# Value units first on un-normalised tiles, and the second block's post norm per token half

## What is computed

```python
def rms_norm(x, g):
    y = x * lax.rsqrt(jnp.mean(x * x, axis=-1, keepdims=True) + 1e-6)
    return y * g

# first block
u = rms_norm(h, norm_mix_g)
qa, ka, va, qk_b, vb, ob, ib, fb, ga, gb = split(u @ w_in)
...   # MoBA attention on a, chunkwise mLSTM on b; vb are the values of b
h = h + merged @ w_out
h = h + ffn(rms_norm(h, norm_ffn_g))
x = rms_norm(h, norm_final_g)

# second block
...   # three kinds of attention, gated and merged
x = x + rmsnorm(merged @ w_out_2, g_mix_post_2)
h = rmsnorm(x, g_ffn_pre_2)
gu = h @ w_ffn_in_2
f = (silu(gu[..., :2816]) * gu[..., 2816:]) @ w_ffn_out_2
x = x + rmsnorm(f, g_ffn_post_2)
```

## Time and profile before

| | |
|---|---|
| median of three runs | 1768.71 us (1766.45 to 1770.39) |
| the profiled execution | 1765.62 us, its span 1763.8 us |
| TensorE busy, weight loads busy | 1722.6 us (98%), 1360.6 us (77%) |
| VectorE, GpSimd, ScalarE busy | 855.0, 671.0, 628.8 us |

### The profile page before, as it was taken

The page is one execution under the profiler, slowest core; times in us unless marked ns, Lnnn a source line. Parts: engine busy times, 40 slices in busy tenths (PEclk is TensorE's granted clock), DMA queues, the critical chain, the costliest instruction groups (busy, mean ns, idle before and its releaser), DMA issues.

```text
span 1763.8 us, 23221 instructions
## 1 busy us (share of the span) xinstructions
PE 1722.6 (98%) x7974; PEld 1360.6 (77%) x7982; DVE 855.0 (48%) x1375; ACT 628.8 (36%) x1011; POOL 671.0 (38%) x284
## 2 busy tenths in 40 slices
PE   7999999999999999999999999999999899999998
PEld 5788776788888888888688665678888588888887
DVE  6602665583655552207497766441332565555013
ACT  5233445433322223327424555453223422222122
POOL 2444222234444444445243000224444444444443
PEclk9999999999999999999999999999999899999999
DMA  4434311123333223334332111113233132233332
GB/s 171 156 121 129 103 53 61 49 96 96 119 95 95 95 96 100 93 102 147 111 96 72 48 37 38 60 49 96 95 100 93 47 118 95 95 95 96 96 97 70
DMA packets 47345, 162.26 MB, mean 92 GB/s; under 512 B 5692, under 2 KB 7868, under 8 KB 47016
## 3 DMA queue, kind: packets, MB, share of 16 engines
q1 hardware_dynamic: 43728, 151.16, 27.1%
q10 hardware_dynamic: 3544, 10.13, 1.7%
HBM read 156.91 MB, written 4.76 MB: 92 GB/s over the span
## 4 chain that ended last, share of the span: by engine, by line
PE 66%; issue 20%; POOL 6%; DVE 5%; ACT 1%; DMA 0%; SPq 0%; POOLq 0%; DVEq 0%; ACTq 0%
PE ps L441 19%; PE ps L443 19%; PE ps L442 19%; POOL w_lo L388 6%; PE ps L908 1%; PE ps L907 1%; PE ps L909 1%; PE ps L606 1%; PE ps L627 1%; PE ps L643 1%; PE ps L795 1%; DVE tmp L1548 1%; DVE tmp L1975 1%; PE ps L837 0%; DMA w_raw<-stream 0%
## 5 line engine op out<-in xcount | busy, mean ns | idle before, releaser
L388 POOL TENSOR_TENSOR w_lo<-w_raw,w_hi 128x1024 fp32r<-128x1024 f32 x267 | 658.5, 2469 | 1066.2 <-ACT w_hi L978 1066.2
L441 PE MATMUL ps<-u_hi,w_hi 128*128 128x512 f32 x1376 | 557.4, 405 | 17.6 <-DVE u_lo L1578 5.7
L443 PE MATMUL ps<-u_hi,w_lo 128*128 128x512 f32 x1376 | 538.6, 391 | 0.0
L442 PE MATMUL ps<-u_lo,w_hi 128*128 128x512 f32 x1376 | 538.1, 391 | 0.0
L978 ACT ACTIVATE w_hi<-w_raw 128x1024 fp32r<-128x1024 f32 x278 | 292.6, 1055 | 413.7 <-PE ps L443 338.4
L441 PEld LDWEIGHTS ps<-u_hi,w_hi 128*128 128x128 f32 x1376 | 259.5, 189 | 95.2 <-issue 41.8
L443 PEld LDWEIGHTS ps<-u_hi,w_lo 128*128 128x128 f32 x1376 | 259.3, 188 | 55.2
L442 PEld LDWEIGHTS ps<-u_lo,w_hi 128*128 128x128 f32 x1376 | 259.7, 189 | 52.4 <-issue 2.6
L1869 DVE TENSOR_TENSOR a_lo<-tmp,a_hi 128x512 f32 (+1 forms) x44 | 116.4, 2646 | 4.7
L1319 ACT ACTIVATE tmp<-tmp 128x512 f32<-128x512 f32 x44 | 27.8, 633 | 222.6 <-DVEq L1859 222.6
L441 PE MATMUL ps<-a_hi,w_hi 128*128 (+1 forms) x264 | 102.9, 390 | 0.0
(11 more groups left out here) (332 smaller groups left out, 2268.7 us busy)
## 6 DMA issues: line engine op xcount, KB each, us to landing
w_raw<-stream SPq DMA_DIRECT2D x278, 512.0 KB, 3.5
g_rep<-g_one ACTq DMA_DIRECT2D x1, 2560.0 KB, 15.4
hT<-xT SPq DMA_DIRECT2D x4, 512.0 KB, 5.4
spread<-m_rows ACTq DMA_DIRECT2D x4, 512.0 KB, 4.8
tmp<-tmp ACTq DMA_DIRECT2D x32, 64.0 KB, 3.8
bias<-g_rep ACTq DMA_DIRECT2D x1, 2048.0 KB, 10.7
outT<-hT SPq DMA_DIRECT2D x16, 128.0 KB, 1.8
mem_in<-memT ACTq DMA_DIRECT2D x1, 1024.0 KB, 4.8
```

What stands on the lines that cost most here:

```text
L388: pool.tensor_tensor(w_lo[:, slot], w_raw[:, slot], w_hi[:, slot].bitcast(F32), ALU.subtract)\
L441: pe.matmul(out, wh, xh, start=start, stop=False)
L442: pe.matmul(out, wh, xl, start=False, stop=False)
L443: return pe.matmul(out, wl, xh, start=False, stop=stop)
```

## The change

Two places. In the first block the section "vb" comes first in the weight stream and runs on un-normalised tiles (x times the norm's gain, split into `first_hi` and `first_lo`), tokens on the partitions; the sums of squares, over tokens as a column too, are made after three of its four units, and 1/rms is applied when ScalarE copies a value bank out (`vb_copy`). SyncE loads a first half weight tile, then x and weights in turns; the vectors come over ScalarE's queue; VectorE makes the low part of the first three weight units. "gif" and "qkb" follow with the normalised tiles as before; the bias matmuls go behind the first pair of units; the gate rows go behind the last convolution, and row transfers behind the bias broadcast, into "ob".

In the second block the last three units of out2 run first for tokens 0 to 255, then for 256 to 511; the post norm is made and applied per token half; three units of ffn2 are fed into buffers of their own (`fw_hi`, `fw_lo`) and run in halves and in halves of k; squares of `n_ffn2` go to a buffer per tile; its sums come in one matmul. Units 3 and 4 are split ahead of that norm's root.

```diff
--- before.py
+++ after.py
 R = 3
 AHEAD = R - 1
 STAGES = [
-    ("gif", 1), ("qkb", 8), ("vb", 4), ("ob", 4), ("va", 4), ("qa", 4), ("ka", 4),
+    ("vb", 4), ("gif", 1), ("qkb", 8), ("ob", 4), ("va", 4), ("qa", 4), ("ka", 4),
...
+            sp.dma_start(w_raw[:, 0, 0:T], stream[0, :, 0:T]).then_inc(loads["w_first"], 16)
+            sp.dma_start(hT[:, 0], xT[:, 0]).then_inc(loads["x0"], 16)
+            sp.dma_start(w_raw[:, 0, T:2 * T], stream[0, :, T:2 * T]).then_inc(landed[0], 16)
+            sp.dma_start(hT[:, 1], xT[:, 1]).then_inc(loads["x1"], 16)
+            sp.dma_start(hT[:, 2:4], xT[:, 2:4]).then_inc(loads["x2"], 16)
+            sp.dma_start(w_raw[:, 1], stream[1]).then_inc(landed[1], 16)
+            for k in (4, 6):
+                sp.dma_start(hT[:, k:k + 2], xT[:, k:k + 2]).then_inc(loads[f"x{k}"], 16)
+            sp.dma_start(w_raw[:, 2], stream[2]).then_inc(landed[2], 16)
+            sp.dma_start(kept[:], tabs[:, 0:KEPT]).then_inc(loads["kept"], 16)
...
+            ring(BY_VECTOR[1], FIRST["ffn2"])
+            for j in range(3):
+                t = FIRST["ffn2"] + j
+                pool.wait_ge(hi_ready, t + 1)
+                pool.tensor_tensor(fw_lo[:, j], w_raw[:, t % R], fw_hi[:, j].bitcast(F32), ALU.subtract)\
+                    .then_inc(lo_ready, 1)
+            for half, cols in enumerate(HALVES):
+                for k in range(1, KT):
+                    pool.wait_ge(*of_norm("n_ffn2", "sq", KT * half + k + 1))
+                    if k >= 2:
+                        pool.wait_ge(*of_norm("n_ffn2", "add", (KT - 1) * half + k - 1))
+                    pool.tensor_tensor(ffn_sq[:, 0, cols], ffn_sq[:, 0, cols], ffn_sq[:, k, cols], ALU.add)\
+                        .then_inc(named("norm_add"), 1)
+            pool.wait_ge(lo_ready, FIRST["ffn2"] + 4)
+            ring(FIRST["ffn2"] + 4, UNITS)
...
+            def first_unit(j, order):
+                for k2, i in order:
+                    k, x = 2 * j + k2, slice(i * P, i * P + P)
+                    if j == 0 and k2 == 0:
+                        pe.wait_ge(named("first_w_lo"), 1)
+                        acquire(VB_BANKS[i])
+                    else:
+                        pe.wait_ge(lo_ready, j + 1)
+                    pe.wait_ge(named("first_lo"), k + 1)
+                    m = split_mm(ps[:, VB_BANKS[i], :], first_hi[:, k, x], first_lo[:, k, x],
+                                 w_hi[:, j % R, k2 * T:k2 * T + T], w_lo[:, j % R, k2 * T:k2 * T + T],
+                                 k == 0, k == KT - 1)
+                    if k == KT - 1 and i < 3:
+                        m.then_inc(named("vb_ready"), 1)
+                m.then_inc(w_used, 1)
+            for j in range(4):
+                first_unit(j, list(product(range(2), range(QT))) if j < 3 else
+                           [(k2, i) for i in range(QT) for k2 in range(2)])
+                if j == 2:
+                    pe.wait_ge(loads["kept"], 16)
+                    acquire(2)
+                    acquire(3)
+                    pe.wait_ge(*of_norm("n_mix", "add", KT - 1))
+                    for q in range(QT):
+                        pe.matmul(ps[:, 3, 4 * q:4 * q + 4], first_sq[:, q * P:q * P + P], ones[:, 0:4],
+                                  start=True, stop=True)
+                    pe.matmul(ps[:, 2, :], ones, first_sq[:, :], start=True, stop=True).then_inc(named("norm_ms"), 1)
+            two_units(FIRST["gif"], u_hi, u_lo, T, ("n_mix", "lo"))
...
-            tokens("vb", [2, 3, 4, 5], u_hi, u_lo)
...
-            tiles_loop("out2", 8, m2_hi, m2_lo, ready=named("m2_lo_done"), banks=out_banks)
-            norm("n_post2", T)
...
-            tiles_loop("ffn2", 44, u_hi, u_lo, ("n_ffn2", "lo"), before_each=mean_square_2, banks=ffn_banks)
+            u = FIRST["out2"]
+            two_units(u, m2_hi, m2_lo, T, named("m2_lo_done"), banks=(4, 5))
+            for j in (2, 3, 4):
+                tile_unit(u + j, (u + j) % R, j % 2, m2_hi, m2_lo)
+            def half_norm(half):
+                acquire(2)
+                pe.wait_ge(named("post2_add"), 3 * half + 3)
+                pe.matmul(ps[:, 2, 0:HALF], ones, tmp[2][:, HALVES[half]], start=True, stop=True)\
+                  .then_inc(named("norm_ms"), 1)
+            for half, cols in enumerate(HALVES):
+                for j in (5, 6, 7):
+                    t, b = u + j, HALF_BANKS[3 * half + j - 5]
+                    pe.wait_ge(lo_ready, t + 1)
+                    acquire(b)
+                    for k in range(KT):
+                        if half == 1 and j == 5 and k == 5:
+                            half_norm(0)
+                        c = slice(k * P, k * P + P)
+                        m = split_mm(ps[:, b, 0:HALF], w_hi[:, t % R, c], w_lo[:, t % R, c], m2_hi[:, k, cols],
+                                     m2_lo[:, k, cols], k == 0, k == KT - 1)
+                    m.then_inc(named("out2_a") if half == 0 else w_used, 1)
+            def ffn2_part(j, half, ks):
+                t, b, cols = FIRST["ffn2"] + j, FIRST_FFN2[j], HALVES[half]
+                if half == 0 and ks[0] == 0:
+                    pe.wait_ge(lo_ready, t + 1)
+                    acquire(b)
+                for k in ks:
+                    pe.wait_ge(*of_norm("n_ffn2", "lo", KT * half + k + 1))
+                    c = slice(k * P, k * P + P)
+                    m = split_mm(ps[:, b, cols], fw_hi[:, j, c], fw_lo[:, j, c], u_hi[:, k, cols],
+                                 u_lo[:, k, cols], k == 0, k == KT - 1)
+                if half == 1 and ks[-1] == KT - 1:
+                    m.then_inc(w_used, 1)
+            front, back = range(KT // 2), range(KT // 2, KT)
+            ffn2_part(0, 0, front)
+            ffn2_part(1, 0, front)
+            half_norm(1)
+            ffn2_part(0, 0, back)
+            ffn2_part(1, 0, back)
+            ffn2_part(2, 0, range(KT))
+            for j in range(3):
+                ffn2_part(j, 1, front)
+            ffn2_part(0, 1, back)
+            ffn2_part(1, 1, back)
+            acquire(2)
+            pe.wait_ge(*of_norm("n_ffn2", "add", 2 * (KT - 1)))
+            pe.matmul(ps[:, 2, :], ones, ffn_sq[:, 0], start=True, stop=True).then_inc(named("norm_ms"), 1)
+            ffn2_part(2, 1, back)
+            pe.wait_ge(named("post2_x_scaled"), 2 * KT)
+            pe.wait_ge(named("post2_x"), 2 * KT)
+            tiles_loop("ffn2", 44, u_hi, u_lo, None, banks=ffn2_banks, made=3)
...
-                    if j > 0:
+                    if j >= fed:
                         feed_after(u + j)
...
+            act.dma_start(vec[:], vecs).then_inc(loads["vec"], 16)
...
+            rs_col = tmp[5][:, 0:4 * QT]
+            def vb_copy(i):
+                if i < 3:
+                    act.wait_ge(named("vb_ready"), i + 1)
+                else:
+                    act.wait_ge(w_used, FIRST["vb"] + 4)
+                own.step(act.activation(vb[:, i], ps[:, VB_BANKS[i], :], ACT.Copy, scale=rs_col[:, 4 * i:4 * i + 1]))
+                act.sem_inc(bank_free[VB_BANKS[i]], 1)
+                act.sem_inc(named("vb_copied"), 1)
+            act.wait_ge(loads["w_first"], 16)
+            act.activation(w_hi[:, 0, 0:T], w_raw[:, 0, 0:T], ACT.Copy).then_inc(named("first_w_hi"), 1)
+            act.wait_ge(loads["vec"], 16)
+            first_raw(0)
+            act.wait_ge(landed[0], 16)
+            act.activation(w_hi[:, 0, T:2 * T], w_raw[:, 0, T:2 * T], ACT.Copy).then_inc(hi_ready, 1)
+            for k in range(1, 4):
+                first_raw(k)
+            feed(1, 1, 0)
+            for k in range(4, KT):
+                first_raw(k)
+            feed(2, 2, 0)
+            for k in range(KT):
+                if k == 4:
+                    feed(3, 3 % R, 3 // R)
+                first_square(k)
+            feed(4, 4 % R, 4 // R)
+            feed(5, 5 % R, 5 // R)
             act.wait_ge(named("set"), 1)
+            act.wait_ge(*of_norm("n_mix", "ms", 1))
+            own.step(act.activation(rs_col, ps[:, 3, 0:4 * QT], ACT.Ln, scale=1.0 / DM, bias=small[:, 8:9]))
+            act.sem_inc(bank_free[3], 1)
+            root("n_mix", T, dst=norm_rs)
+            own.step(act.activation(rs_col, rs_col, ACT.Exp, scale=-0.5))
             for k in range(KT):
-                if k % 2 == 0:
-                    act.wait_ge(loads[f"x{k // 2}"], 16)
-                act.activation(first_sq[:, k], hT[:, k], ACT.Square).then_inc(named("norm_sq"), 1)
-            for t in range(AHEAD):
-                feed(t, t, 0)
-            root("n_mix", T, dst=norm_rs)
-            feed(AHEAD, AHEAD, 0)
-            norm_hi("n_mix", u_hi, T)
+                norm_hi_tile("n_mix", u_hi, T, k)
+                if k == 3:
+                    vb_copy(0)
+                if k == 4:
+                    vb_copy(1)
+            vb_copy(2)
+            vb_copy(3)
+            feed(6, 6 % R, 6 // R)
...
+            half_square(0)
+            feed_ffn2(0)
+            half_square(1)
```

(69 more changed lines are left out.)

221 lines of the change are left out of this document (143 added, 78 removed).

## The result

The changed kernel takes **1753.25 us** (median of 4 runs, 1752.91 to 1754.88) against 1767.58 for the kernel before beside it (4 runs, 1766.28 to 1770.39): a ratio of 0.9919, 95% interval 0.9901 to 0.9936, so faster by 14.3 us. The two profiled executions lie closer together: 1765.62 before, 1754.88 after, 10.7 us. There are two questions: which steps of that sum were right, and why the medians lie further apart than the profiles.

The account below looks back on a forecast made before the run. TensorE, busy 98% of the span, was taken as the bound. Gains of 4.9 us up to "ob" and 5.7 at ffn2's unit 5, 10.6 together, gave 1755.0 profiled and 1758.2 as the forecast; range 1753.5 to 1763.5.

Parts of the forecast that it names:

- a wait of 3.7 for the two copies: First block, after the value units: TensorE idles 3.7 us until ScalarE has copied banks 0 and 1 out.
- Rival (a): Start of the kernel: transfers land later, first matmul at 9.5 not 6.5, three us lost, 1761.2; chance 0.13.
- rival (d): Value units: the 1.2 GHz clock lasts through them, 85 more slow matmuls, 17 us, 1775, slower; chance 0.05.
- rival (b): ffn2: VectorE's half tiles slower beside GpSimd's adds, pair 0 at 1403.6, unit 5 at most 2.7 early, 1761.2; chance 0.11.
- (c): Late transfers and slow half tiles together, or a late feed behind the broadcast: 1766, no change to be told; chance 0.09.
- TensorE waits 2.0 us and 1.4 us: First three units of ffn2: waits for the fourth and eighth half tiles; the three units end at 1400.2.
- pair 0 starts there: ffn2, VectorE: pair 0 starts when the norm's root is done, at 1400.5.
- pair 1 at 1409.4: ffn2, VectorE: pair 1 starts at 1409.4, 8.85 us between pairs as before; unit 5's weights are ready at 1414.6.
- Up to 'ob': First block, from the pair after the value units: "ob" starts at 89.0 against 93.93, a gain of 4.9 us.
- since the gate rows now follow the last convolution: First block, seven units before "ob": the reason given for the 2.44 us stall going away.
- Idles of 2.69 and 3.12 us were followed by slow matmuls, one of 2.44 was not: First block: ground for charging 2.2 us of slow clock behind the 3.7 us idle after the value units.
- 1758.1 beside the median: Whole kernel: 1755.0 for the profiled execution, carried to the median, which lay 3.1 us above the profile before.

Follow-up runs that it names:

- copies_early: Changed kernel with ScalarE's copies out of banks 0 and 1 behind the first and second normalised tile instead of the fourth and fifth: 1747.44 us.
- kept_busy: Changed kernel with sixteen 512-column matmuls that nobody reads added on TensorE between the value units and the gif pair: 1751.88 us.
- pool_yields_2: Kernel before, gate rows left between the convolutions, with two waits added on GpSimd so its low parts follow VectorE's row subtractions: 1763.37 us, ratio 0.9983.
- rows_last: Kernel before with only the gate rows moved behind VectorE's last convolution, and their transfers later: 1763.57 us, ratio 0.9980.
- vb_only: Kernel before with only the first half of the change, everything up to "ob"; second block's post norm as before: 1759.77 us, ratio 0.9952.
- feed_between: Changed kernel with ScalarE feeding unit 5 of ffn2 between the sigmoids of pairs 0 and 1 instead of behind the latter: 1752.7 us, one run.
- both_better: Changed kernel with bank copies behind tiles one and two, fourteen zero matmuls at the start, two norm copies on ScalarE, unit 5 fed before the root: 1743.99 us.

## Why the prediction was right, and where it was not

**Right, in the first block.** First matmul 6.5, found 6.42; value units to 32.2, found 32.15 and its slot; a wait of 3.7 for the two copies, found 3.69; slow clock behind it, found, 13 matmuls for the 11 taken; "ob" 4.9 us earlier, found 4.5. copies_early and kept_busy show both terms of that wait to be what I took them for. Rival (a) fell at the first row; rival (d), the slow clock through the value units, by their granted clock, 1.00 from 11.30 to 32.38; rival (b) at unit 5, and (c) with them.

**Right in sum, wrong in two terms: ffn2.** The times of the changed kernel here plus 4.7 us stand in the frame of the kernel before, as the prediction's do. "TensorE waits 2.0 us and 1.4 us", 3.4 together, was 4.2, in four pieces. Each piece costs some 0.4 us beyond its idle, since the streams of 0.12 us a matmul break off and start again: by the distances of starts the four cost 5.3 us and two smaller ones 0.6, 5.9 where I had 3.4. So the three units end at 1403.1 (1398.41 and 4.7) for a forecast of 1400.2, and pair 0 starts at 1403.35 (1398.66 and 4.7), where I had "pair 0 starts there", 1400.5, 2.9 us earlier. Rival (b), pair 0 at 1403.6 since VectorE's half tiles take longer beside GpSimd's adds, was right on this link, in the number and in part in the reason: six of the low parts of half tiles begin 0.1 to 0.2 us behind an addition of squares on GpSimd and take 0.86 to 0.91 us for 0.47, 2.6 us together. How much of TensorE's waits comes from these, no run separates. But "pair 1 at 1409.4" was found at 1408.9. I had taken the 8.85 us between the pairs from the earlier trace rows; 3.3 of these are the two operations that GpSimd holds, and with no feed between the two sigmoids GpSimd has nothing to do there: 5.5 us. That the two errors cancel is luck. Unit 5 starts at 1414.2 for a forecast of 1414.6, and its expected wait of 3.5 us is not there, since TensorE itself is free only 0.15 us earlier.

**The steps that failed.** First, "Up to 'ob'": the sum of the first block ended there, and everything behind it was taken as shifted as it stood. Another 1.8 us lay 95 us later, in a wait of 2.2 at the first attention that no step spoke of. It went because VectorE's addition no longer starts under GpSimd's low part. Second, the reason given for the lost 2.44 us stall, "since the gate rows now follow the last convolution": pool_yields_2 shows that the rows could have stayed. Third, "Idles of 2.69 and 3.12 us were followed by slow matmuls, one of 2.44 was not": true of that execution, not of the kernel. rows_last gains 3.3 us in the median by a stall of 2.44 in the trace, so the slow clock behind it is worth about 0.9 on average, and I counted nothing. (The 0.9 is an estimate; the interval of rows_last allows 1.9 to 5.1 us for the 3.3.) Fourth, "1758.1 beside the median": I carried the 3.1 us between the profiled execution and the median of three runs over to the changed kernel. In five sets of runs the kernel before lies 0.5 to 2.0 above its profiled execution, and the changed one 1.0 to 1.6 below its own, which had lost 1.65 in B.

The fourth weighs most: the sum for the profiled execution was met, 1755.0 for 1754.88 (1.5 and 0.3 us too little, 1.65 too much), and nearly all of the 4.95 us between 1758.2 and 1753.25 is the offset, 3.1 up where it was 1.6 down.

With these the medians come out: 4.5 up to "ob", 1.8 at the attention, 0.9 of clock behind the old stall and 5.4 in C are 12.6 us, and the averages of A and C over several executions, 8.1 and 5.4, are 13.5; the two comparisons gave 14.3 and 12.3. With the first step's 1.8 us in the sum and an offset of 0.5 to 2.0 us the forecast would have been 1753.7 to 1755.2. What was not settled: why the turning transfers land 1 to 1.8 us later in some kernels than in others, and at which place the clock parts the two groups of vb_only.

## What to carry to other kernels

Before taking a duration from a trace, look at what the other engine that shares its memory port was doing in it: an operation of VectorE that takes 0.7 us in one row and 2.7 in the next is not two operations but one that was held, and a change that only moves one of the two engines' work can win or lose that time far from where it was made. An engine with slack that shares a port with one that has none can be made to wait for it; here that gave 1.3 and 3.4 us. And a wait of 1.5 to 2.5 us of TensorE has no one price: read its clock in several executions before counting on it, and try giving the matrix engine something to do in an idle that cannot be removed (2.0 and 2.2 us here).

## What was not expected of the hardware

- A subtraction on 4 partitions of 512 columns is held by GpSimd as long as one on 128 partitions (2.76 and 2.75 us, 0.68 and 0.69 when free). What counts is GpSimd's operation, 2.4 us, not VectorE's size.
- The slow clock came behind every idle of 3.1 to 3.7 us (six of six normalised-tile waits of 3.1 to 3.4, five of five copy waits of 3.69) and by chance behind shorter ones: 4 of 16 behind the wait of 1.5 at 996 to 1013, 3 of 8 behind the one of 1.6 in ffn2, 2 of 4 behind the stall of 2.44 to 2.48, 1 of 6 behind the wait of 2.2 to 2.8 at the first attention. It need not start at once: in feed_between five matmuls behind the 3.69 us run 0.23 apart, and then the granted clock is 0.50 from 36.40 to 39.70. The Trainium skill ("TensorE: Matmul & The Clock Gate", part 1) says that the same kernel shows 6, 11 or 14 slow matmuls from run to run; the first stream of split matmuls had from some 7 to 14 in the traces here that do not start with zeros.
- Fourteen matmuls of bfloat16 zeros took 5.04 us and left the clock fast for the first split matmul (granted 1.00 from 6.10 in both_better, which has them too): zeros counted as work for it.
